# Two expert layers: first stage on a ring of eight tiles loaded by pairs, and 18 weighted row sums per layer moved to the value stage

## Chip, cores and metric

The kernel runs on one core of one Trainium2 chip. The metric is the device time of one execution in microseconds; the figure before is the median of three runs.

## What is computed

The program is a chain of a hybrid first layer, an even layer (sparse attention), an expert layer, an MLA layer, a second expert layer and a final norm, all over 256 tokens of width 1024. The change touches the two expert layers alone. Cut to them, the reference is:

```
def peer_ffn(h, w_q, sub_keys, u_tab, v_tab):      # u_tab, v_tab: 128*128 experts x 1024
    q = (xc @ w_q).reshape(t, 8, 2, 128)
    sc = einsum('thpc,hpnc->thpn', q, sub_keys)
    v_half, i_half = top_k(sc, 16)                 # 16 of 128 first keys, 16 of 128 second keys
    top_s, pos = top_k(all 16*16 sums, 16)         # 16 experts for each of 8 heads
    g = softmax(top_s)
    act = gelu(einsum('thkd,td->thk', u_tab[expert], xc))
    return einsum('thk,thkd->td', g * act, v_tab[expert])
```

## The kernel before

An expert layer (`expert_layer`, once with i = 0 and once with i = 1) treats 192 of the 256 tokens densely and 64 by gathers.

**Dense tokens, first stage.** For each of 128 first keys, TensorE multiplies the key's tile of u (128 x 1024 floats, 0.5 MB) with the tokens: `experts`, L2401, eight matmuls of 192 columns into half a bank. For each pair of keys ScalarE applies the gelu and stores into `hidden` (L2504). VectorE meanwhile finds the 16 experts of each head, and after key 80 the weights begin: VectorE writes one-hots (`one_hots`, L2280 to L2286), TensorE multiplies them (`weights`, L2296, 32 products of 6 tokens over keys 0 to 79 of `hidden`), VectorE multiplies the result into `hidden` (`weigh`, L2305).

**Dense tokens, value stage.** For each of 128 tiles of v (0.5 MB), ScalarE rounds the tile (`tile_hi`, L2491 and L2523) and the key's row of `hidden` (`w_parts`, L2495, L2496), VectorE makes the two remainders (`value_rest`: `tile_lo` L2729, `w_parts` L2732), and TensorE does ten matmuls of 512 columns (`values`: L2428, L2429, L344 to L346). Over the first 72 tiles, 24 weight products of the other 48 keys lie among them, one behind each third tile, with their one-hots and weighings on VectorE.

**The 64 other tokens.** GpSimd gathers 128 times 0.5 MB through eight buffers (L2245): 64 u rows, with each of which VectorE makes a dot product (`row_dot`, L2253), and 64 v rows, each of which VectorE weights and adds (`row_value`, L2259, called a weighted row sum or sum below). `take(upto)` places them in VectorE's order, up to a count: `TAKEN[3]` of the 128 are done when the first stage ends, `TAKEN[4]` after value tile index 72 of the loop, and the rest is spread evenly up to index `LAST_TAKE`. A gather waits until the buffer's last row is used.

**Loads.** SyncE issues all tiles in order into a ring of four slots in `wbuf`. A u tile's load waits until the key four before is used by TensorE (semaphore `used`); a v tile's load waits until VectorE has made the remainder of the tile four before (`lo_done`). `tile_hi` and `tile_lo` lie behind the ring in `wbuf` and aren't used in the first stage.

**Order at the turn of the stages.** On ScalarE, behind the gelu of keys 124 and 125, v tiles 0 and 1 are rounded. When the last key is used and the weighing is done, the hidden rows of four tiles are rounded, then comes the last gelu, then v tiles 2 and 3.

Every engine works through its own queue in order, written out by hand; only semaphores tie them together.

Of the kernel before, what the change touches and what calls it, by code (L numbers as in the profile page):

```python
# [119 lines left out]
def build(nc, ins, out):  # L120
    with ExitStack() as ctx:
# [24 lines left out]
        def carver():  # L146
# [1960 lines left out]
def expert_layer(nc, g, ins, i):  # L2107
# [112 lines left out]

    def sync(sp):
# [8 lines left out]
        load_table(sp, U, M_U, lo_done, used)  # L2230
# [3 lines left out]
        load_table(sp, V, M_V, used, lo_done)  # L2234
# [73 lines left out]
    FIRST_WEIGHING, FIRST_LOOPS, FIRST_LOOP = FIRST_KEYS // STEP, 2, 20  # L2308
    FIRST_AT = {j: n for n, j in enumerate(j for j in range(FIRST_LOOP) if j % 5 < 4)}
# [3 lines left out]
    TAKEN, LAST_TAKE = (16, 30, 36, 86, 92), 118  # L2313
    EXPS_AT, ACTS_AT, ACTS = (16, 30), (46, 51), (slice(0, 48), slice(48, SHARED))
# [21 lines left out]
    def tensor(pe):  # L2336
# [627 lines left out]
```

## Time and profile before

| | |
|---|---|
| median of 3 runs | 2057.09 us (2050.85 to 2057.55) |
| the profiled execution | 2056.46 us, span 2054.4 us |
| TensorE busy (PE), weight loads (PEld) | 97%, 87% |
| VectorE, ScalarE, GpSimd busy | 78%, 42%, 18% |
| moved over the span | 511.18 MB, mean 249 GB/s |
| the 4096 records of L2401 | 683.8 us busy |
| the 128 weighted row sums, L2259 | 164.2 us busy, 1283 ns each |
| u and v loads | 256 of 512.0 KB each, median 6.3 and 4.7 us to landing |

The time of an execution is a little over the span, which is from the first to the last instruction. An instruction's duration can overlap the next one on its engine, so the cost of one in a row of many is the distance from start to start.

### The profile page before, as it was taken

Reading aid. Unit: us, or ns where it says so; the run is one execution under the profiler, and the core shown is the slowest. Engines: PE = TensorE matmul, PEld = TensorE weight load, DVE = VectorE, ACT = ScalarE, POOL = GpSimd, SP = SyncE. Lnnn points to the kernel's source line nnn. Section 1 sums busy time; section 2 is a strip of 40 time slices with the busy share of each in tenths; the row PEclk is TensorE's granted clock in tenths of the full one; section 3 lists DMA queues with packets and bytes.
Section 4 is the critical chain, followed back from the end, with each engine's and each line's share of the span. In section 5 each row is a group of like instructions: output and inputs, shape, how many; then the busy total and the mean of one; then the engine's idle time right before and its main releaser. Section 6 shows DMA issues by size and latency. Waiting matters only on the chain.

```text
span 2054.4 us, 35333 instructions
## 1 busy us (share of the span) xinstructions
PE 2001.3 (97%) x12408; PEld 1792.1 (87%) x12408; DVE 1607.6 (78%) x3302; ACT 863.2 (42%) x1655; POOL 377.9 (18%) x262
## 2 busy tenths in 40 slices
PE   8999999999999999999999999999999999999998
PEld 6888887879999999988888787899999999888886
DVE  6899886865798159868889977649951996988997
ACT  6557555555101100056566666531101001655665
POOL 0000000000024225500125200000341453011460
PEclk9999999999999999999999999999999999999999
DMA  6554335415389979976779853335997899777895
GB/s 252 207 182 186 113 122 161 155 36 196 125 337 361 351 253 391 374 245 233 235 249 395 326 197 124 106 125 201 396 372 270 326 380 347 234 235 235 322 397 201
DMA packets 132636, 511.18 MB, mean 249 GB/s; under 512 B 15005, under 2 KB 15133, under 8 KB 129857
## 3 DMA queue, kind: packets, MB, share of 16 engines
q1 hardware_dynamic: 95680, 375.81, 51.7%
q0 software_dynamic: 36864, 134.23, 17.1%
q8 instruction: 48, 0.79, 0.1%
q14 instruction: 44, 0.35, 0.0%
HBM read 508.94 MB, written 1.05 MB: 248 GB/s over the span
## 4 chain that ended last, share of the span: by engine, by line
PE 66%; DVE 17%; DMA 2%; ACT 2%; issue 2%; SPq 0%; DVEq 0%; ACTq 0%
PE bank L2401 22%; PE bank L344 10%; PE bank L346 10%; PE bank L345 10%; PE bank L2428 5%; PE bank L2429 5%; DVE e_gbuf L2253 3%; DVE x_tok L2259 3%; DVE e_hot_first L2286 2%; DVE e_hidden L2305 2%; DMA wbuf<-in_peer_v 2%; PE bank L2296 1%; DVE e_is_first L2280 1%; DVE e_hot_second L2282 1%; DVE tile_lo L274 1%
## 5 line engine op out<-in xcount | busy, mean ns | idle before, releaser
L2401 PE MATMUL bank<-h_dense,wbuf 128*128 128x192 f32 x4096 | 683.8, 327 | 3.2 <-ACT e_stage L2477 2.4
L2401 PEld LDWEIGHTS bank<-h_dense,wbuf 128*128 128x128 f32 x4096 | 663.4, 190 | 6.2 <-issue 4.3
L2523 ACT ACTIVATE tile_hi<-wbuf 128x1024 fp32r<-128x1024 f32 x248 | 263.8, 1064 | 225.6 <-PE bank L346 139.9
L2729 DVE TENSOR_TENSOR tile_lo<-wbuf,tile_hi 128x1024 fp32r<-128x1024 f32 x256 | 312.9, 1222 | 44.2 <-ACT tile_hi L2491 34.3
L2504 ACT ACTIVATE e_hidden<-bank 128x384 f32<-128x384 f32 x128 | 62.9, 492 | 609.9 <-PE bank L2401 609.9
L2245 POOL DMA_INDIRECT e_gbuf<-in_peer_v,e_row_at x128 | 224.4, 1753 | 489.4 <-DVE x_tok L2259 465.5
L2245 POOL DMA_INDIRECT e_gbuf<-in_peer_rows,e_row_at x128 | 151.4, 1183 | 476.5 <-DVE e_dots L2253 261.3
L2428 PE MATMUL bank<-tile_hi,w_parts 128*128 128x512 f32 x512 | 205.4, 401 | 4.0 <-DVE w_parts L2732 3.8
L274 DVE TENSOR_TENSOR tile_lo<-wbuf,tile_hi 128x1024 fp32r<-128x1024 f32 (+2 forms) x117 | 140.5, 1212 | 76.3 <-ACT tile_hi L266 75.5
L2429 PE MATMUL bank<-tile_lo,w_parts 128*128 128x512 f32 x512 | 200.1, 391 | 0.0
L344 PE MATMUL bank<-tile_hi,w_parts 128*128 128x512 f32 x512 | 199.7, 390 | 0.0
L345 PE MATMUL bank<-tile_lo,w_parts 128*128 128x512 f32 x512 | 199.6, 390 | 0.0
L346 PE MATMUL bank<-tile_hi,w_parts 128*128 128x512 f32 x512 | 199.5, 390 | 0.0
L355 PE MATMUL bank<-a_parts,tile_hi 128*128 128x512 f32 x512 | 181.0, 399 | 0.0
L2253 DVE CUSTOM_DVE_ANT_0 e_gbuf<-e_gbuf,x_gathered 128x1024 f32<-128x1024 f32 x128 | 152.9, 1222 | 17.2 <-DMA e_gbuf<-in_peer_rows,e_row_at 16.8
L2259 DVE SCALAR_TENSOR_TENSOR x_tok<-e_gbuf,e_acts,x_tok 128x1024 f32<-128x1024 f32 x128 | 164.2, 1283 | 1.8
L266 ACT ACTIVATE tile_hi<-wbuf 128x1024 fp32r<-128x1024 f32 (+2 forms) x117 | 122.1, 1047 | 64.5 <-PE bank L346 57.5
L354 PE MATMUL bank<-a_parts,tile_hi 128*128 128x256 f32 x512 | 144.2, 282 | 0.4 <-DVE tile_hi L681 0.2
L2239 POOL MEMSET x_tok<- 64x1024 f32 x2 | 1.9, 950 | 660.9 <-DVE e_stage L2560 660.9
L2428 PEld LDWEIGHTS bank<-tile_hi,w_parts 128*128 128x128 f32 x512 | 96.2, 188 | 26.7 <-DVE w_parts L2732 7.6
L561 ACT ACTIVATE tile_hi<-wbuf 128x512 fp32r<-128x512 f32 x144 | 90.3, 632 | 69.4 <-PE bank L355 65.8
L681 DVE TENSOR_TENSOR tile_hi<-wbuf,tile_hi 128x512 fp32r<-128x512 f32 x144 | 98.5, 688 | 24.5 <-ACT tile_hi L561 23.6
(396 smaller groups left out, 3472.2 us busy)
## 6 DMA issues: line engine op xcount, KB each, us to landing
wbuf<-in_peer_u SPq DMA_DIRECT2D x256, 512.0 KB, 6.3
wbuf<-in_peer_v SPq DMA_DIRECT2D x256, 512.0 KB, 4.7
wbuf<-in_w_in SPq DMA_DIRECT2D x16, 2048.0 KB, 7.8
wbuf<-in_peer_q SPq DMA_DIRECT2D x32, 512.0 KB, 3.8
wbuf<-in_hyb_in SPq DMA_DIRECT2D x16, 512.0 KB, 3.6
wbuf<-in_mla_uq SPq DMA_DIRECT2D x9, 512.0 KB, 3.4
wbuf<-in_mla_in SPq DMA_DIRECT2D x8, 528.0 KB, 4.6
wbuf<-in_w_v SPq DMA_DIRECT2D x2, 2048.0 KB, 7.2
```

The costliest lines, as they stand in the source:

```text
L344: nc.tensor.matmul(out, hi[:, cols], other_hi, start=start, stop=False, **kw)
L345: nc.tensor.matmul(out, hi[:, cols], other_lo, start=False, stop=False, **kw)
L346: return nc.tensor.matmul(out, lo[:, cols], other_hi, start=False, stop=stop, **kw)
L355: return nc.tensor.matmul(out, hi[:, cols], parts, start=False, stop=stop, skip_group_check=True)
L2245: nc.gpsimd.indirect_dma_start(out=gbuf[:, b, :], out_offset=None, in_=(U_ROWS if n < SHARED else V_ROWS)[:, :], in_offset=bass.IndirectOf ...
L2253: nc.vector.tensor_tensor_reduce(out=gbuf[:, n % GBUFS, :], in0=gbuf[:, n % GBUFS, :], in1=x_gathered[:, :], scale=1.0, scalar=0.0, op0=AL ...
L2259: nc.vector.scalar_tensor_tensor(out=x[:, 1, :], in0=gbuf[:, n % GBUFS, :], scalar=acts[:, n:n + 1], in1=x[:, 1, :], op0=ALU.mult, op1=ALU ...
L2401: last = nc.tensor.matmul(bank[:, j // 2 % 2, j % 2 * S:j % 2 * S + DENSE], ring[:, slot, k * P:(k + 1) * P], h_dense[:, k, :], start=(k = ...
L2428: nc.tensor.matmul(sums(1, c), both, tile_hi[:, slot, cols], start=False, stop=False, skip_group_check=True)
L2429: last = nc.tensor.matmul(sums(1, c), both, tile_lo[:, slot, cols], start=False, stop=False, skip_group_check=True)
L2523: nc.scalar.activation(tile_hi[:, slot, 0:D], ring[:, slot, 0:D], ACT.Copy).then_inc(hi_done, 1)
L2729: nc.vector.tensor_tensor(tile_lo[:, slot, 0:D], ring[:, slot, 0:D], tile_hi[:, slot, 0:D].bitcast(F32), ALU.subtract).then_inc(lo_done, 1)
```

## The change

1. `deep` is a ring of eight u tiles over the memory of the old ring and of `tile_hi`. `load_pair` fills two neighbouring tiles with one transfer of 1 MB, `experts` waits for it at every even key, and `load_first` refills a pair when both its keys are used. V tiles keep the ring of four; the first four of them are loaded behind keys 120, 122, 124 and 126.
2. At the turn ScalarE waits for the weighing behind the gelu of keys 124 and 125, then rounds v tile 0, its hidden row, v tile 1, its hidden row; tiles 2 and 3 with their rows follow the last gelu.
3. The 32 weight products of the first stage lie behind three of four keys from key 80 to 111 and behind two of three from key 112 to 122, before behind four of five keys from 80 to 119.
4. `TAKEN` places 68 of the gathered rows in the first stage instead of 86: of the 64 weighted row sums, 4 instead of 22. Value tiles to index 72 get 10 instead of 6, the rest 50 instead of 36, over 49 indices instead of 46.

```diff
+            "deep": wbuf[:, 0:2, :].rearrange("p w (j c) -> p (w j) c", c=TILE),
...
-    def load_table(sp, table, base, before, free):
-
-        for j in range(STEP):
-            sp.wait_ge(before if j < SLOTS else free, base + j - SLOTS + 1)
-            load_slot(sp, table, j, (base + j) % SLOTS)
-        with sp.Fori(1, ROUNDS) as r:
-            for j in range(STEP):
-                sp.wait_ge(free, STEP * r + base + j - SLOTS + 1)
-                load_slot(sp, table, STEP * r + j, (base + j) % SLOTS)
+    def load_pair(sp, a, p):
+        sp.dma_start(deep[:, 2 * p:2 * p + 2, 0:D], U[bass.ds(a, 2), :, :].rearrange("a p c -> p a c")).then_inc(ring_loaded[p], DMA)
+
+    def load_first(sp):
+        for p in range(SLOTS):
+            ring_slots = [s % SLOTS for s in (2 * p, 2 * p + 1)]
+            if p < SLOTS // 2:
+                sp.wait_ge(lo_done, max(last_before(s) for s in ring_slots + [p]) + 1)
+            else:
+                sp.wait_ge(lo_done, last_before(p) + 1)
+                sp.wait_ge(used, max(last_before(s) for s in ring_slots) + 1)
+            load_pair(sp, 2 * p, p)
+        with sp.Fori(1, ROUNDS) as r:
+            for p in range(SLOTS):
+                sp.wait_ge(used, STEP * r + M_U - STEP + 2 * p + 2)
+                load_pair(sp, STEP * r + 2 * p, p)
...
+    def load_second(sp):
+        for a in range(SLOTS):
+            slot = (M_V + a) % SLOTS
+            sp.wait_ge(used, M_U + LAST_ROUND + 2 * slot + 1)
+            load_value(sp, a, slot)
+        for a in range(SLOTS, STEP):
+            sp.wait_ge(lo_done, M_V + a - SLOTS + 1)
+            load_value(sp, a, (M_V + a) % SLOTS)
...
-    FIRST_WEIGHING, FIRST_LOOPS, FIRST_LOOP = FIRST_KEYS // STEP, 2, 20
-    FIRST_AT = {j: n for n, j in enumerate(j for j in range(FIRST_LOOP) if j % 5 < 4)}
+    FIRST_WEIGHING, FIRST_LOOPS, FIRST_LOOP = FIRST_KEYS // STEP, 2, 2 * STEP
+    FIRST_AT = {j: n for n, j in enumerate(j for j in range(FIRST_LOOP) if j % 4 < 3)}
+    FIRST_END = FIRST_KEYS + FIRST_LOOPS * FIRST_LOOP
+    END_AT = {j: FIRST_LOOPS * len(FIRST_AT) + n for n, j in enumerate(j for j in range(12) if j % 3 < 2)}
...
-    TAKEN, LAST_TAKE = (16, 30, 36, 86, 92), 118
-    EXPS_AT, ACTS_AT, ACTS = (16, 30), (46, 51), (slice(0, 48), slice(48, SHARED))
+    TAKEN, LAST_TAKE = (16, 30, 36, 68, 78), 121
+    EXPS_AT, ACTS_AT, ACTS = (16, 30), (51, 61), (slice(0, 48), slice(48, SHARED))
...
-            slot = (M_U + j) % SLOTS
-            pe.wait_ge(ring_loaded[slot], DMA * (width // SLOTS * q + (M_U + base + j) // SLOTS + 1))
+            slot = (base + j) % STEP
             if j % 2 == 0:
+                pe.wait_ge(ring_loaded[slot // 2], DMA * (width // STEP * q + pairs_loaded(slot // 2) + (base + j) // STEP + 1))
...
             act.wait_ge(used, M_U + 2 * f + 2)
-            if f == NKEYS // 2 - 1:
-                act.wait_ge(weighted, 2 + NGROUPS[0])
-                for a in range(SLOTS):
-                    hidden_rounded(a, a)
...
             if f >= NKEYS // 2 - 2:
-                for a in range(2):
-                    rounded_v(2 * (f - NKEYS // 2 + 2) + a)
+                if f == NKEYS // 2 - 2:
+                    act.wait_ge(weighted, 2 + NGROUPS[0])
+                for e in range(2):
+                    a = 2 * (f - NKEYS // 2 + 2) + e
+                    rounded_v(a)
+                    hidden_rounded(a, a)
```

Line numbers of the changed kernel are larger: L2729 becomes L2768, L2732 L2771, L2259 L2291, L2504 L2539.

VectorE in the value stage of the first expert layer, near tile 90, before (x_tok is the weighted row sum):

```order
L2729 TENSOR_TENSOR tile_lo<-wbuf,tile_hi 128x1024 [waits hi_done]
L2732 TENSOR_TENSOR w_parts<-e_hidden,w_parts 128x192 [waits e0_w_hi_done]
L2259 SCALAR_TENSOR_TENSOR x_tok<-e_gbuf,e_acts,x_tok 128x1024 [waits gather_used,gathered1]
L2729 TENSOR_TENSOR tile_lo<-wbuf,tile_hi 128x1024 [waits hi_done]
L2732 TENSOR_TENSOR w_parts<-e_hidden,w_parts 128x192 [waits e0_w_hi_done]
L2729 TENSOR_TENSOR tile_lo<-wbuf,tile_hi 128x1024 [waits hi_done]
L2732 TENSOR_TENSOR w_parts<-e_hidden,w_parts 128x192 [waits e0_w_hi_done]
```

The same place in the changed kernel:

```order
L2768 TENSOR_TENSOR tile_lo<-wbuf,tile_hi 128x1024 [waits hi_done]
L2771 TENSOR_TENSOR w_parts<-e_hidden,w_parts 128x192 [waits e0_w_hi_done]
L2291 SCALAR_TENSOR_TENSOR x_tok<-e_gbuf,e_acts,x_tok 128x1024 [waits gather_used,gathered7]
L2768 TENSOR_TENSOR tile_lo<-wbuf,tile_hi 128x1024 [waits hi_done]
L2771 TENSOR_TENSOR w_parts<-e_hidden,w_parts 128x192 [waits e0_w_hi_done]
L2291 SCALAR_TENSOR_TENSOR x_tok<-e_gbuf,e_acts,x_tok 128x1024 [waits gather_used,gathered0]
```

Before, some tiles have no sum ahead of them (36 sums over 46 tiles); in the changed kernel each of the tiles 74 to 122 has one, and tile 123 has two.

ScalarE at the turn of the stages in the first expert layer, before, from the gelus up to that of keys 124 and 125 (eleven in one row) to the last rounding ahead of the value loop (left out are the hidden rows of tiles 1 to 3):

```order
L2504 ACTIVATE e_hidden<-bank 128x384 [waits used] x11
L2491 ACTIVATE tile_hi<-wbuf 128x1024 [waits ring_loaded0]
L2491 ACTIVATE tile_hi<-wbuf 128x1024 [waits ring_loaded1]
L2495 ACTIVATE w_parts<-e_hidden 128x192 [waits e0_weighted,used]
L2496 ACTIVATE w_parts<-e_hidden 128x64
...
L2504 ACTIVATE e_hidden<-bank 128x384
L2491 ACTIVATE tile_hi<-wbuf 128x1024 [waits ring_loaded2]
L2491 ACTIVATE tile_hi<-wbuf 128x1024 [waits ring_loaded3]
```

And in the changed kernel:

```order
L2539 ACTIVATE e_hidden<-bank 128x384 [waits used]
L2530 ACTIVATE tile_hi<-wbuf 128x1024 [waits ring_loaded0,used,e0_weighted]
L2534 ACTIVATE w_parts<-e_hidden 128x192
L2535 ACTIVATE w_parts<-e_hidden 128x64
L2530 ACTIVATE tile_hi<-wbuf 128x1024 [waits ring_loaded1,used]
L2534 ACTIVATE w_parts<-e_hidden 128x192
L2535 ACTIVATE w_parts<-e_hidden 128x64
L2539 ACTIVATE e_hidden<-bank 128x384 [waits used]
```

The hidden rows of tiles 0 and 1 have moved ahead of the last gelu and no longer wait for the last key; the wait for the weighing moved up with them.

## Rows read from the trace of the kernel before

**Rows 1.** Timeline of ScalarE, the gelu of a pair of keys: start us, duration us.
```profile
542.75 0.49 ACT L2504 ACTIVATE e_hidden<-bank 128x384 f32<-128x384 f32 x1 [3.37 <-PE bank L2401]
...
589.55 0.49 ACT L2504 ACTIVATE e_hidden<-bank 128x384 f32<-128x384 f32 x1 [4.71 <-PE bank L2401]
...
741.74 0.49 ACT L2504 ACTIVATE e_hidden<-bank 128x384 f32<-128x384 f32 x1 [4.71 <-PE bank L2401]
748.49 0.49 ACT L2504 ACTIVATE e_hidden<-bank 128x384 f32<-128x384 f32 x1 [6.25 <-PE bank L2401]
...
778.62 0.49 ACT L2504 ACTIVATE e_hidden<-bank 128x384 f32<-128x384 f32 x1 [5.22 <-PE bank L2401]
...
880.29 0.49 ACT L2504 ACTIVATE e_hidden<-bank 128x384 f32<-128x384 f32 x1 [4.71 <-PE bank L2401]
...
1396.72 0.49 ACT L2504 ACTIVATE e_hidden<-bank 128x384 f32<-128x384 f32 x1 [3.37 <-PE bank L2401]
...
1734.48 0.49 ACT L2504 ACTIVATE e_hidden<-bank 128x384 f32<-128x384 f32 x1 [4.84 <-PE bank L2401]
```

**Rows 2.** Chain that ended last, then timeline of TensorE, first stage.
```profile
592.56 8.18 DMA wbuf<-in_peer_u
...
830.33 0.62 PE L2296 MATMUL bank<-e_hot_first,e_hot_second 128*128 128x80 f16 x12 [0.31 <-DVE e_hot_first L2286]
```

**Rows 3.** Timeline of TensorE at the turn, both layers; idle time stands in brackets.
```profile
888.08 0.70 PE L2428 MATMUL bank<-tile_hi,w_parts 128*128 128x512 f32 x1 [2.62 <-DVE w_parts L2732]
...
892.07 0.57 PE L2296 MATMUL bank<-e_hot_first,e_hot_second 128*128 128x48 f16 x16
892.49 0.47 PE L2428 MATMUL bank<-tile_hi,w_parts 128*128 128x512 f32 x1
...
1740.63 0.50 PE L2428 MATMUL bank<-tile_hi,w_parts 128*128 128x512 f32 x1 [0.99 <-DVE w_parts L2732]
...
1743.87 0.47 PE L2428 MATMUL bank<-tile_hi,w_parts 128*128 128x512 f32 x1
```

**Rows 4.** Timeline of TensorE: first matmuls of tiles 73, 127; 73, 114, 127.
```profile
1067.83 0.39 PE L2428 MATMUL bank<-tile_hi,w_parts 128*128 128x512 f32 x1
...
1192.56 0.39 PE L2428 MATMUL bank<-tile_hi,w_parts 128*128 128x512 f32 x1
...
1919.21 0.39 PE L2428 MATMUL bank<-tile_hi,w_parts 128*128 128x512 f32 x1
...
2012.14 0.39 PE L2428 MATMUL bank<-tile_hi,w_parts 128*128 128x512 f32 x1
...
2042.45 0.39 PE L2428 MATMUL bank<-tile_hi,w_parts 128*128 128x512 f32 x1
```

**Rows 5.** Windows: length, busy PE, PEld, DVE, ACT, POOL; clock, DMA share, GB/s.
```profile
888.00:892.50 4.50, 4.42 (x27) 3.40 (x27) 4.50 (x11) 3.31 (x9) 0.00 (x0) 0.62 0.81 304
...
1100.00:1131.00 31.00, 31.00 (x138) 25.63 (x137) 30.53 (x37) 19.07 (x40) 16.44 (x11) 1.00 1.01 394
...
1917.00:2034.00 117.00, 116.91 (x514) 95.94 (x513) 115.36 (x141) 74.51 (x153) 60.70 (x29) 1.00 0.95 357
```

**Rows 6.** Timeline of VectorE: a weighing cycle, tile 73, tiles 84 and 85.
```profile
1046.48 0.56 DVE L2305 SCALAR_TENSOR_TENSOR e_hidden<-bank,e_hidden 128x384 f32<-128x384 f32 x1 [0.95 <-PE bank L2296]
...
1915.52 0.35 DVE L2732 TENSOR_TENSOR w_parts<-e_hidden,w_parts 128x192 fp32r<-128x192 f32 x1
...
1939.39 1.23 DVE L2729 TENSOR_TENSOR tile_lo<-wbuf,tile_hi 128x1024 fp32r<-128x1024 f32 x1
...
1940.80 1.29 DVE L2259 SCALAR_TENSOR_TENSOR x_tok<-e_gbuf,e_acts,x_tok 128x1024 f32<-128x1024 f32 x1
1941.99 1.23 DVE L2729 TENSOR_TENSOR tile_lo<-wbuf,tile_hi 128x1024 fp32r<-128x1024 f32 x1
```

**Rows 7.** Chain that ended last, value stage of the first expert layer.
```profile
1068.40 7.04 DMA wbuf<-in_peer_v
...
1075.53 1.07 ACT tile_hi L2523
```

More of the change, by code:

```diff
@@ L2229, in sync @@
             load_tile(sp, g, ins, M_Q + j)
-        load_table(sp, U, M_U, lo_done, used)
+        load_first(sp)
         if i == 0:
@@ L2233, in sync @@
                 sp.sem_clear(handle)
-        load_table(sp, V, M_V, used, lo_done)
+        load_second(sp)
     def gpsimd(pool):
@@ L2394, in experts @@
         def experts(q, width, base, j):
-            slot = (M_U + j) % SLOTS
-            pe.wait_ge(ring_loaded[slot], DMA * (width // SLOTS * q + (M_U + base + j) // SLOTS + 1))
+            slot = (base + j) % STEP
             if j % 2 == 0:
+                pe.wait_ge(ring_loaded[slot // 2], DMA * (width // STEP * q + pairs_loaded(slot // 2) + (base + j) // STEP + 1))
+                if base + j >= LAST_ROUND:
+                    pe.sem_inc(ring_loaded[slot // 2], NKEYS // STEP * DMA)
                 pe.wait_ge(bank_free, width // 2 * q + (base + j) // 2 + 1)
             for k in range(KT):
-                last = nc.tensor.matmul(bank[:, j // 2 % 2, j % 2 * S:j % 2 * S + DENSE], ring[:, slot, k * P:(k + 1) * P], h_dense[:, k, :],
+                last = nc.tensor.matmul(bank[:, j // 2 % 2, j % 2 * S:j % 2 * S + DENSE], deep[:, slot, k * P:(k + 1) * P], h_dense[:, k, :],
                                         start=(k == 0), stop=(k == KT - 1))
@@ L2416, in tensor @@
                     weights(pe, 0, len(FIRST_AT) * q + FIRST_AT[j], FIRST_AT[j] % 2)
-        for j in range(NKEYS - FIRST_KEYS - FIRST_LOOPS * FIRST_LOOP):
-            experts(0, STEP, FIRST_KEYS + FIRST_LOOPS * FIRST_LOOP, j)
+        for j in range(NKEYS - FIRST_END):
+            experts(0, STEP, FIRST_END, j)
+            if j in END_AT:
+                weights(pe, 0, END_AT[j], END_AT[j] % 2)
         def values(q, width, base, j, ends=False):
@@ L2489, in rounded_v @@
             slot = (M_V + a) % SLOTS
+            act.wait_ge(used, M_U + NKEYS - SLOTS + slot + 1)
             act.wait_ge(ring_loaded[slot], DMA * ((M_V + a) // SLOTS + 1))
```

12 lines of the change are left out of this document (10 added, 2 removed).

## Prediction

> **What bounds the kernel now.** I read the stage windows first, then followed each stage's pace by one instruction that recurs in it, then looked only at where the pace breaks. TensorE is the bound almost everywhere, so a term counts only where TensorE waits.
>
> First stage: the gelu (L2504) starts once per pair of keys. Its starts at 542.75 and 589.55 us are nine pairs apart, 5.20 us each [rows 1]. From 748.49 to 778.62 lie five pairs and eight weight products of L2296: 30.13 - 26.00 = 4.13, or 0.516 us each [rows 1]. The pair from 741.74 to 748.49 takes 6.75, which is 5.20 + 0.52 + 1.02 for turning the picks, work that stays. So 61 pairs should take 61 x 5.20 + 32 x 0.516 + 1.02 = 334.7 us. They take 880.29 - 542.75 = 337.5 in the first expert layer and 1734.48 - 1396.72 = 337.8 in the second [rows 1]. The stalls are thus 2.8 and 3.1 us. Two kinds make them: a late u tile (the chain that ended last goes through a landing of 8.18 us at 592.56) and late one-hots from VectorE (TensorE idle 0.31 before 830.33) [rows 2].
>
> Turn from first to value stage: TensorE idles 2.62 us in the first layer, and the value tile behind it takes 892.49 - 888.08 = 4.41 us; in the second layer 0.99, and 1743.87 - 1740.63 = 3.24 [rows 3].
>
> Value stage: from tile 73 to tile 114 of the second layer, 41 tiles, TensorE needs 2012.14 - 1919.21 = 92.9 us, 2.267 each [rows 4]. VectorE is the engine to watch: it is busy 115.36 of 117 us in the last third of this stage [rows 5]. A tile with a row sum takes it 1941.99 - 1939.39 = 2.60 us, and the sum alone 1941.99 - 1940.80 = 1.19 (1.20 below) [rows 6]. A tile without one is 1.40. So VectorE is slower than TensorE on a tile with a sum (by 0.33) and faster on one without (by 0.87). What saves TensorE is a lead: the parts of tile 73 are ready at 1915.52 + 0.35 = 1915.87 [rows 6], and TensorE wants them at 1919.21 [rows 4], 3.34 us later. Before, 36 sums lie over 46 tiles and the lead is used up only near the end: tiles 73 to 127 should take 54 x 2.267 = 122.4 and take 124.7 in the first layer (1192.56 - 1067.83) and 123.2 in the second (2042.45 - 1919.21) [rows 4]. That is 2.3 and 0.8 us lost.
>
> **Part one, the ring and the pairs.** A slot of four is refilled when its key is used, so a load has three keys, 7.8 us, to land; 8.18 didn't fit [rows 2]. A pair in a ring of eight has six keys, 15.6 us. The pair is one transfer of 1 MB instead of two of 0.5; even at twice the 8.18 us it would be late by under 1 us. Its issue costs SyncE less, and nothing queues behind it there except the next pair. I take the u stalls as gone.
>
> **Part two, fewer sums in the first stage.** A weight product there now comes each 4/3 key (3.98 us) and later each 1.5 keys, before each 1.25 keys (3.77). VectorE's share falls from 50/32 = 1.56 sums per product to 1. Its wait for nothing and TensorE's 0.31 at 830.33 [rows 2] say that it was just over budget; 0.56 x 1.20 = 0.67 us less work in 0.2 us more time clears it. With part one: gain 2.8 + 3.1 = **5.9 us**, bounds 3 (one of the two kinds stays; these rows don't split them, so I take half) and 5.9, since no more stall exists.
>
> **Part three, the turn.** The v loads now leave after keys 120, 122, 124 and 126, and ScalarE rounds v tiles 0 and 1 and their hidden rows right behind the gelu of keys 124 and 125, 5.2 us before the last key ends. ScalarE needs 0.49 for the gelu [rows 1] and 1.07 for a tile [rows 7], VectorE 1.4 more, so both tiles are ready before TensorE is. The new wait for the weights stands ahead of this on ScalarE; behind it are the last gelu and the v roundings. It asks for product 31, which is made after key 122, three keys earlier, so it costs nothing; were it late, the gain of the turn shrinks by that much. A usual value tile with its weight product is 2.27 plus 892.49 - 892.07 = 0.42 [rows 3], 2.69. So the turn costs 2.62 + 4.41 - 2.69 = 4.3 and 0.99 + 3.24 - 2.69 = 1.5 us; I keep 0.2 each for the switch of code. Gain 4.1 + 1.3 = **5.4 us**, bounds 3.6 (the two idles alone) and 5.8. Most of the first layer's excess is the clock: granted 0.62 of full in 888.00:892.50 after the long idle [rows 5], a mix of the 1.2 and 2.4 GHz levels. With no idle nothing drops it.
>
> **Part four, 18 more sums in the value stage.** Four go to tiles 0 to 73, where weight products leave VectorE 0.95 us of waiting in a cycle of three tiles [rows 6]. Ten sums over 24 cycles, never two in one: 0.25 of each is taken from the lead, which the next cycle's 0.95 gives back, so nothing. If it didn't come back, it would be 10 x 0.25 = 2.5 us per layer. The other 14 are the price. The order listing has one sum ahead of each of tiles 74 to 122, and two ahead of tile 123. VectorE needs 49 x 2.60 + 3.80, TensorE 50 x 2.267: behind by 49 x 0.333 + 1.53 = 17.9 us. The lead pays 3.3, so TensorE loses 14.6 us per layer. Less what it loses already: 14.6 - 2.3 + 14.6 - 0.8 = **26.1 us**. What covered a sum, the tiles without one between, is gone. Behind tile 123 no sum follows, but VectorE's later slack can't give time back to TensorE.
>
> The lower bound of this term is a sum hidden by something I don't see; I find no row for that, since every sum takes 1.20. The upper bound is the transfers. A v tile and a gather in 2.60 us are 1.049 MB, or 403 GB/s. The window 1100.00:1131.00 moved 394 GB/s at a share of 1.01 [rows 5], and a v tile then needed 7.04 us to land [rows 7], where the ring of four allows 4 x 2.60 less 1.07 and 1.40, 7.9. At 394, a tile takes 2.66: 0.06 x 42 tiles = 2.5 us per layer more, 5 in all. I take 1.
>
> The Trainium skill (DMA: Bandwidth & Descriptors, Where 436 GB/s comes from) says that for transfers between HBM and SBUF the HBM side binds at about 358 GB/s per core. By that rule a tile of 1.049 MB would take 2.93 us and the two tails some 28 us more than my sum. The row with 394 GB/s speaks against it here.
>
> **Sum.** -5.9 - 5.4 + 26.1 + 1 = +15.8. The profiled execution is 2056.46 us (span 2054.4), the median 2057.09, 0.6 above it. 2056.5 + 15.8 = 2072.3, and 2072.9 beside the median: I say 2073.
>
> **Rivals.**
> A, as above, VectorE paces both tails: with the bounds of the other terms 2057.1 + 26.1 - 11.7 = 2071 to 2057.1 + 26.1 + 5 - 6.6 = 2082, and some 4 us below for what my reading of the lead and of the sum may be off. Chance 0.77.
> B, the transfers pace the tails. For it: the share of 1.01. Against: 394 GB/s is 2% short of 403, eight gather buffers smooth it, and VectorE's slower pace asks for less per us in the v ring. At 394 GB/s: 2077. At the 357 GB/s that 1917.00:2034.00 moved [rows 5], which wasn't asked for more, 2.94 us per tile: 0.34 x 42 x 2 = 28 more, 2100. Chance 0.11, mostly its lower half.
> C, TensorE's clock falls in the tails, since TensorE now pauses 0.33 us in every tile. The tile after the long idle took 892.07 - 888.08 = 3.99 instead of 2.27 [rows 3]. That is 1.4 more than VectorE's 2.60; one tile in four of the 39 without lead gives 14 us per layer: 2100. Against: the pause before 830.33 [rows 2] and a last stretch at granted 1.00 [rows 5]. Chance 0.03. The Trainium skill (TensorE: Matmul & The Clock Gate, A second HAM failure mode) describes a kernel whose frequent short idles made the clock oscillate.
> D, the other side: a row sum in the tail costs VectorE less than 1.20. With t for the sum, 49 tiles of 1.40 + t and one of 1.40 + 2t against 50 x 2.267 + 3.3 make TensorE's loss 51t - 46.7 per layer. The rest of the change gives 11.3, and before's loss 3.1, so the balance is at 7.2 per layer, t = 1.06. Below that the kernel is faster: at t = 1.0 by some 6 us, 2051. For it: VectorE would have to be slowed now by something that the change thins out, such as TensorE's or the transfers' traffic. Against: the tail before, with and without a sum, keeps to 2.60 and 1.40 [rows 6], and gathers become denser, not rarer. Within 0.3%: 0.04, faster: 0.05.
>
> **Numbers.** 0.3% (about 6 us) is what a measurement here tells from no change. A gives 2067 to 2082; the range adds B's nearer half and a little of the ground between A and D: 2064 to 2084. Outside are the far half of B, C and D, 0.05 + 0.03 + 0.09, so under 2 in 10. Faster 0.05, within 0.3% 0.05 (D's 0.04 and an edge of A), slower 0.90.
>
> **What would show it.** First stages: 61 pairs in 334.7 us, no idle named after u. Turn: an idle under 0.3 us and a first tile of 2.7. Tail: tiles 84 to 122 at 2.60 us, each waiting on VectorE, tile 127 of the second layer 137 us after tile 73, VectorE without idle between. Wrong if tail tiles stay at 2.27, if they wait on ScalarE and through it on v landings over 7.9 us (B), if the granted clock dips there (C), or if the first stage shows stalls of a new kind.

## The result, and the profile after

The changed kernel takes 2076.07 us (median of five runs, 2072.78 to 2080.81); the kernel before takes 2057.55 (five runs, 2050.85 to 2061.82). The ratio is 1.0091, with a 95% interval of 1.0075 to 1.0108: slower by 18.5 us. The forecast was 2073, in a range of 2064 to 2084.

The page of the changed kernel: span, then busy time, share and instructions of each engine.

```profile
span 2074.0 us, 34807 instructions
...
PE 2020.3 (97%) x12408; PEld 1789.3 (86%) x12408; DVE 1606.2 (77%) x3302; ACT 861.3 (42%) x1655; POOL 353.4 (17%) x262
```

The totals say next to nothing: the same instructions stand in another order. So here too the stages are laid out by instructions that recur. First the gelu of the changed kernel, timeline of ScalarE, against [rows 1]; the rounding and the hidden row that now stand between the last two gelus are shown with it.

```profile
545.78 0.49 ACT L2539 ACTIVATE e_hidden<-bank 128x384 f32<-128x384 f32 x1 [3.37 <-PE bank L2437]
...
880.64 0.49 ACT L2539 ACTIVATE e_hidden<-bank 128x384 f32<-128x384 f32 x1 [4.61 <-PE bank L2437]
881.02 1.05 ACT L2530 ACTIVATE tile_hi<-wbuf 128x1024 fp32r<-128x1024 f32 x1
881.97 0.35 ACT L2534 ACTIVATE w_parts<-e_hidden 128x192 fp32r<-128x192 f32 x1
...
885.84 0.49 ACT L2539 ACTIVATE e_hidden<-bank 128x384 f32<-128x384 f32 x1 [2.02 <-PE bank L2437]
...
1406.48 0.49 ACT L2539 ACTIVATE e_hidden<-bank 128x384 f32<-128x384 f32 x1 [3.37 <-PE bank L2437]
...
1741.34 0.49 ACT L2539 ACTIVATE e_hidden<-bank 128x384 f32<-128x384 f32 x1 [4.61 <-PE bank L2437]
```

61 pairs take 880.64 - 545.78 = 334.86 us in either layer; they took 337.5 and 337.8 [rows 1]. V tile 0 is rounded at 881.02, 4.5 us before TensorE wants it.

Timeline of TensorE of the changed kernel: value tiles 0, 1 and 73 of the first layer, tiles 92 and 93, the tile with two sums ahead of it (123) and tile 127; then tiles 73 and 127 of the second layer. They answer to [rows 3, 4].

```profile
885.50 0.53 PE L2466 MATMUL bank<-tile_hi,w_parts 128*128 128x512 f32 x1
...
887.95 0.57 PE L2328 MATMUL bank<-e_hot_first,e_hot_second 128*128 128x48 f16 x16
888.37 0.47 PE L2466 MATMUL bank<-tile_hi,w_parts 128*128 128x512 f32 x1
...
1063.71 0.39 PE L2466 MATMUL bank<-tile_hi,w_parts 128*128 128x512 f32 x1
...
1109.83 0.50 PE L2466 MATMUL bank<-tile_hi,w_parts 128*128 128x512 f32 x1
...
1112.43 0.50 PE L2466 MATMUL bank<-tile_hi,w_parts 128*128 128x512 f32 x1
...
1192.14 0.47 PE L2466 MATMUL bank<-tile_hi,w_parts 128*128 128x512 f32 x1 [1.47 <-DVE w_parts L2771]
...
1201.33 0.39 PE L2466 MATMUL bank<-tile_hi,w_parts 128*128 128x512 f32 x1
...
1924.49 0.39 PE L2466 MATMUL bank<-tile_hi,w_parts 128*128 128x512 f32 x1
...
2062.06 0.39 PE L2466 MATMUL bank<-tile_hi,w_parts 128*128 128x512 f32 x1
```

The turn has no idle, and the first value tile takes 888.37 - 885.50 = 2.87 us (before 4.41 and 3.24). Tiles 73 to 127 take 137.6 us in each layer, against 124.7 and 123.2 [rows 4]. Tiles 92 and 93 are 2.60 apart, not 2.27.

Waits of the changed kernel in 1925:2062, the second layer's tail: engine, what it waited for, total us, times, longest; and then its windows there (columns as in [rows 5]).

```profile
ACT tile_hi L2562 <- DMA wbuf<-in_peer_v: 52.9, 46, 2.5
...
PEld bank L2466 <- DVE w_parts L2771: 17.0, 37, 0.7
...
DVE tile_lo L2768 <- ACT tile_hi L2562: 0.3, 1, 0.3
```
```profile
1920.00:2062.00 142.00, 138.91 (x561) 101.88 (x560) 140.31 (x165) 78.74 (x162) 71.20 (x43) 1.00 0.92 355
...
1950.00:2025.00 75.00, 73.87 (x289) 52.02 (x289) 74.96 (x87) 42.40 (x88) 47.78 (x30) 1.00 1.03 409
```

Here the engine that waits for nothing is VectorE: 0.3 us in 137, and 74.96 of 75.00 busy. ScalarE waits long for v tiles, but VectorE waits for ScalarE only once, for 0.3 us, so those 52.9 us cost nothing here. TensorE's weight loads wait for VectorE 37 times.

**Where 19.6 us between the two profiled executions went.** First stages 334.86 - 337.55 and 334.86 - 337.76: -5.6. From the last full gelu to value tile 1: 7.73 in both layers, where it was 12.19 and 9.39: -6.1. Tiles 1 to 73: 175.34 and 175.42, before 175.34 twice: +0.1. Tails: +12.9 and +14.3. This is +15.6. Another 3.0 come from code ahead of the first expert layer which the change doesn't touch: the expert stage starts at 535.08 instead of 532.05, after a stretch in which the two kernels' windows (before first, changed second) show another granted clock.

```profile
400.00:450.00 50.00, 42.67 (x293) 33.02 (x292) 36.81 (x129) 28.41 (x93) 0.00 (x0) 0.86 0.06 19
```
```profile
400.00:450.00 50.00, 42.56 (x278) 32.93 (x277) 35.96 (x128) 28.57 (x93) 0.00 (x0) 0.80 0.06 18
```

The last 1 us is spread over the rest. Below, stages are therefore compared and not spans alone; "tail" is tile 73 to tile 127 by their first matmuls. The sums given for a tail are those that `TAKEN` places behind index 72; one more, the last of those before, also lies behind the parts of tile 73 in every kernel.

### The profile page after: what moved, and what is told of

Read it like the earlier page. It is cut to its first block, busy times and chain, and to the rows that moved or that the text cites. A ratio compares the mean times of both kernels' runs of the same rounds, so it can differ in the third digit from the quotient of the medians.

```text
span 2074.0 us, 34807 instructions
## 1 busy us (share of the span) xinstructions
PE 2020.3 (97%) x12408; PEld 1789.3 (86%) x12408; DVE 1606.2 (77%) x3302; ACT 861.3 (42%) x1655; POOL 353.4 (17%) x262
## 4 chain that ended last, share of the span: by engine, by line
PE 70%; DVE 12%; issue 5%; ACT 2%; DMA 1%; DVEq 0%; ACTq 0%; SPq 0%
PE bank L2437 32%; PE bank L345 8%; PE bank L347 8%; PE bank L346 8%; DVE x_tok L2291 5%; PE bank L2466 4%; PE bank L2467 3%; PE bank L2328 2%; DVE w_parts L2771 1%; DMA wbuf<-in_peer_v 1%; DVE tile_lo L275 1%; PE bank L2420 1%; DVE tile_lo L2768 1%; PE bank L1573 0%; ACT tile_hi L267 0%
## 5 line engine op out<-in xcount | busy, mean ns | idle before, releaser
L2768 DVE TENSOR_TENSOR tile_lo<-wbuf,tile_hi 128x1024 fp32r<-128x1024 f32 x256 | 311.4, 1216 | 23.1 <-ACT tile_hi L2530 17.6
L2539 ACT ACTIVATE e_hidden<-bank 128x384 f32<-128x384 f32 x128 | 62.7, 490 | 607.7 <-PE bank L2437 607.7
L2277 POOL DMA_INDIRECT e_gbuf<-in_peer_v,e_row_at x128 | 205.2, 1603 | 489.3 <-DVE x_tok L2291 441.2
L2277 POOL DMA_INDIRECT e_gbuf<-in_peer_rows,e_row_at x128 | 146.1, 1141 | 534.9 <-DVE e_dots L2285 321.9
L2466 PE MATMUL bank<-tile_hi,w_parts 128*128 128x512 f32 x512 | 213.4, 417 | 6.0 <-DVE w_parts L2771 3.4
L345 PE MATMUL bank<-tile_hi,w_parts 128*128 128x512 f32 x512 | 199.7, 390 | 0.0
L347 PE MATMUL bank<-tile_hi,w_parts 128*128 128x512 f32 x512 | 199.4, 389 | 0.0
L2291 DVE SCALAR_TENSOR_TENSOR x_tok<-e_gbuf,e_acts,x_tok 128x1024 f32<-128x1024 f32 x128 | 163.3, 1275 | 0.3
L2337 DVE SCALAR_TENSOR_TENSOR e_hidden<-bank,e_hidden 128x480 f32<-128x480 f32 (+1 forms) x112 | 68.4, 611 | 79.3 <-PE bank L2328 79.2
```

What stands on the lines that cost most here:

```text
L345: nc.tensor.matmul(out, hi[:, cols], other_hi, start=start, stop=False, **kw)
L347: return nc.tensor.matmul(out, lo[:, cols], other_hi, start=False, stop=stop, **kw)
L2277: nc.gpsimd.indirect_dma_start(out=gbuf[:, b, :], out_offset=None, in_=(U_ROWS if n < SHARED else V_ROWS)[:, :], in_offset=bass.IndirectOf ...
L2291: nc.vector.scalar_tensor_tensor(out=x[:, 1, :], in0=gbuf[:, n % GBUFS, :], scalar=acts[:, n:n + 1], in1=x[:, 1, :], op0=ALU.mult, op1=ALU ...
L2466: nc.tensor.matmul(sums(1, c), both, tile_hi[:, slot, cols], start=False, stop=False, skip_group_check=True)
L2768: nc.vector.tensor_tensor(tile_lo[:, slot, 0:D], ring[:, slot, 0:D], tile_hi[:, slot, 0:D].bitcast(F32), ALU.subtract).then_inc(lo_done, 1)
```

## Experiments

Ten kernels, in three groups on one chip each; the kernel before took 2059.02, 2058.42 and 2057.88 us in them. Unless the text says otherwise, a diff is against the changed kernel. `TAKEN` counts gathers, of which 64 are the dot products: 86 means 22 sums in the first stage.

**Only the sums put back.**

```diff
-    TAKEN, LAST_TAKE = (16, 30, 36, 68, 78), 121
-    EXPS_AT, ACTS_AT, ACTS = (16, 30), (51, 61), ...
+    TAKEN, LAST_TAKE = (16, 30, 36, 86, 92), 118
+    EXPS_AT, ACTS_AT, ACTS = (16, 30), (46, 53), ...
```

> The changed kernel with the old placing of the row sums (86 gathered rows in the first stage, 92 by value tile 72, the rest by index 118); the ring of eight, the pairs and the new turn stay. Theory V (VectorE is late in the tail because of the moved sums): the tail, tile 73 to tile 127, goes back to 123 to 125 us per layer from 137.7, the first stage keeps its 334.8 us for 61 pairs, the turn its 5.2 us, and the kernel is 11 us faster than before, 2046. Rival X (the 1 MB pairs or the deeper ring cost something themselves): it stays at or above 2057, with new idle time in the first stage or the turn.

Measured: 2049.11 us, ratio 0.9958 (0.9940 to 0.9976). Tails 125.8 and 124.5, 61 pairs 334.76 in both layers, although the first stage has its 22 sums again. The loss is in part four alone, and ring, pairs and turn are a gain. The time is 3 us above the 2046 that was expected: the first tail lies 0.8 us above its range, and the first value tile of the second layer took 4.12 us, where that of the first layer took 2.85. Timeline of this kernel, TensorE and then ScalarE at that place:

```profile
1734.00 0.57 PE L2328 MATMUL bank<-e_hot_first,e_hot_second 128*128 128x48 f16 x16 [1.12 <-DVE e_hot_first L2318]
```
```profile
1729.95 1.06 ACT L2530 ACTIVATE tile_hi<-wbuf 128x1024 fp32r<-128x1024 f32 x1 [2.69 <-DMA wbuf<-in_peer_v]
```

V tile 1 landed late, its remainder stands ahead of the next one-hots on VectorE, and TensorE's weight product waited 1.12 us for these.

**Only the sums moved.** The kernel before, with parts one to three left out. Against before:

```diff
-    TAKEN, LAST_TAKE = (16, 30, 36, 86, 92), 118
-    EXPS_AT, ACTS_AT, ACTS = (16, 30), (46, 51), ...
+    TAKEN, LAST_TAKE = (16, 30, 36, 68, 78), 121
+    EXPS_AT, ACTS_AT, ACTS = (16, 30), (51, 60), ...
```

> The kernel before with only the placing of the row sums from the change (68, 78, index 121). Theory V: the tails take 137.7 us instead of 124.7 and 123.2, so +27, and the one-hot waits of the first stage (about half of 5.9) go: -3. Sum +24, 2081. Rival X: within a few us of 2057.

Measured: 2080.21, ratio 1.0102 (1.0087 to 1.0118). Tails 138.4 and 137.6: the old ring and the old turn pay the same price. 61 pairs take 336.04 and 335.42, so fewer sums alone take 1.5 and 2.3 of the 2.8 and 3.1 us of stalls in the first stage. These are mostly the late one-hots: the waits of TensorE's weight loads for them fell from 2.5 us to 0.5 in both layers. In the second layer, those for u tiles fell too, from 1.2 us to 0.2, with the old ring and fewer gathers. TensorE, second layer, tiles 73 and 127:

```profile
1925.92 0.39 PE L2428 MATMUL bank<-tile_hi,w_parts 128*128 128x512 f32 x1
...
2063.54 0.39 PE L2428 MATMUL bank<-tile_hi,w_parts 128*128 128x512 f32 x1
```

**Half of each sum.** This kernel weights and adds only half of each gathered row; gathers and v tiles are all loaded.

```diff
-        nc.vector.scalar_tensor_tensor(out=x[:, 1, :], in0=gbuf[:, n % GBUFS, :], ..., in1=x[:, 1, :],
+        nc.vector.scalar_tensor_tensor(out=x[:, 1, 0:CHUNK], in0=gbuf[:, n % GBUFS, 0:CHUNK], ..., in1=x[:, 1, 0:CHUNK],
```

> The changed kernel, but each weighted row sum treats only columns 0 to 511 of the 1024, so the output lacks the other half of those sums; all gathers stay. Theory V: VectorE needs about 0.6 us less per sum, 2.0 us per tile with a sum, less than TensorE's 2.27, so no tile waits and the tail takes 122.4 to 123.5 us: about -29, 2047. Rival B (the transfers, 403 GB/s asked in the tail, pace it, VectorE's work is only beside them): at 2.27 us per tile the same bytes would be 462 GB/s, which no window has shown, so the tail stays above 2.5 us per tile at first and ScalarE waits for v tiles; a tail of 130 us or more.

Measured: 2064.5, ratio 1.0029 (1.0018 to 1.0039), tails 132.3 and 132.4. Windows of this kernel in the second layer's tail, then timelines of ScalarE and VectorE there:

```profile
1950.00:2025.00 75.00, 74.35 (x297) 53.21 (x296) 63.84 (x90) 43.04 (x88) 51.94 (x30) 1.00 1.03 409
```
```profile
1978.29 1.06 ACT L2562 ACTIVATE tile_hi<-wbuf 128x1024 fp32r<-128x1024 f32 x1 [1.10 <-DMA wbuf<-in_peer_v]
...
1980.79 1.06 ACT L2562 ACTIVATE tile_hi<-wbuf 128x1024 fp32r<-128x1024 f32 x1 [1.04 <-DMA wbuf<-in_peer_v]
```
```profile
1978.24 0.75 DVE L2291 SCALAR_TENSOR_TENSOR x_tok<-e_gbuf,e_acts,x_tok 128x512 f32<-128x512 f32 x1
...
1979.38 1.23 DVE L2768 TENSOR_TENSOR tile_lo<-wbuf,tile_hi 128x1024 fp32r<-128x1024 f32 x1 [0.40 <-ACT tile_hi L2562]
```

VectorE now has 63.84 us of work in 75, so it needs about 2.2 us per tile and waits 0.40 for ScalarE, which waits over 1 us for each v tile. At 409 GB/s a tile with its gather, 1.049 MB, takes 2.56 us. TensorE keeps to this: by its timeline, tiles 90 to 118 of the second layer are (2032.11 - 1960.46) / 28 = 2.56 us apart.

```profile
1960.46 0.50 PE L2466 MATMUL bank<-tile_hi,w_parts 128*128 128x512 f32 x1
...
2032.11 0.50 PE L2466 MATMUL bank<-tile_hi,w_parts 128*128 128x512 f32 x1
```

This is the bound that comes next, and it lies 0.04 us under VectorE's 2.60. With VectorE relieved, the tails fall by 5 us, not to 122: 2064.5 is 17 us above the 2047 that was expected, and the tails are those that the rival of this run named, 130 us or more with ScalarE waiting for v tiles. So VectorE sets the pace of the changed kernel, but some 10 of the 15 us that each of its tails loses to TensorE's pace would stay if VectorE alone were faster.

**The sums back, and six more between weighings.** 22 sums in the first stage, 12 in tiles 0 to 73, 30 in the tail.

```diff
-    TAKEN, LAST_TAKE = (16, 30, 36, 68, 78), 121
+    TAKEN, LAST_TAKE = (16, 30, 36, 86, 98), 118
```

(`ACTS_AT` is (46, 53), as in the first experiment.)

> The changed kernel with 86 gathered rows in the first stage, 12 sums by value tile 72 and only 30 in the tail (to index 118). Theory V: VectorE needs 46 x 1.40 + 30 x 1.20 = 100.4 us where TensorE needs 104.3, so the lead is never used up and the tail takes 122.4 to 123.0 us; with the first stage and the turn of the change the kernel is 14 us faster than before, 2043. Rival X: at or above 2057. Rival Y (the first stage can't hold 86 rows without the one-hot waits even with the products farther apart): 3 us of stalls in the first stages, 2046.

Measured: 2048.03, ratio 0.9942 (0.9927 to 0.9957). This is 5 us above the 2043 expected. Tails 125.4 and 126.9, not under 123. Windows of this kernel's second tail, and a rounding in it:

```profile
1914.00:2034.00 120.00, 119.09 (x512) 94.67 (x511) 109.01 (x133) 72.71 (x152) 31.16 (x22) 1.00 0.88 314
```
```profile
1955.53 1.06 ACT L2562 ACTIVATE tile_hi<-wbuf 128x1024 fp32r<-128x1024 f32 x1 [3.16 <-DMA wbuf<-in_peer_v]
```

VectorE has 11 us of slack in 120, and still TensorE loses 3 to 4.5. What is late are v tiles: ScalarE waits up to 3.16 us for one, VectorE for ScalarE (10.8 us in all), TensorE for VectorE. A count of VectorE's work alone misses this.

**Fourteen more sums between weighings.** The 14 sums come out of the tail (50 to 36) into tiles 0 to 73 (10 to 24, one in each weighing cycle); first stage and turn are those of the changed kernel.

```diff
-    TAKEN, LAST_TAKE = (16, 30, 36, 68, 78), 121
+    TAKEN, LAST_TAKE = (16, 30, 36, 68, 92), 118
```

> The changed kernel with its 68 gathered rows in the first stage, but 24 of the 60 sums among tiles 0 to 72 (one in each cycle of three, instead of 10) and 36 in the tail, to index 118, as before. Theory V (the loss is where the sums lie, not that they are in the value stage): the tail goes back to about 125.5 us as in the run with the old placing; a cycle of three tiles has 1.15 us of waiting on VectorE for a sum of 1.20, so tiles 1 to 73 take 175.3 to 178 us. Sum 2049 to 2054. Rival Z (18 more sums in the value stage cost about 27 us wherever they lie, since stage and bytes are the same): 2070 or more.

Measured: 2049.85, ratio 0.9960 (0.9945 to 0.9974). Tiles 1 to 73 take 175.34 and 175.36, as without these sums; tails 124.7 and 128.4, the second 3 us above the 125.5 expected. TensorE, second layer, tiles 1 and 73:

```profile
1736.01 0.47 PE L2466 MATMUL bank<-tile_hi,w_parts 128*128 128x512 f32 x1
...
1911.37 0.39 PE L2466 MATMUL bank<-tile_hi,w_parts 128*128 128x512 f32 x1
```

The 14 sums cost nothing between weighings, and their absence takes 12.9 and 9.1 us off the tails. In the second layer they used up some of the lead, though: the parts of tile 73 are ready 2.87 us before TensorE starts it, and 3.33 in the first layer. In that tail VectorE waits 6.0 us for ScalarE, which waits up to 4.15 us for a v tile.

**Seven sums out of the tail.** A dose between the two: 43 sums in the tail.

```diff
-    TAKEN, LAST_TAKE = (16, 30, 36, 68, 78), 121
+    TAKEN, LAST_TAKE = (16, 30, 36, 68, 85), 121
```

> The changed kernel with 85 instead of 78 gathered rows done by value tile 72, so 17 sums among tiles 0 to 72 and 43 in the tail (to index 121). VectorE's bound by the prediction's sum: 7 sums of 1.20 less in the tail, a loss of 14.6 - 8.4 = 6.2 us per layer instead of 14.6, tail 128.6 us instead of 137.7 at best; transfers at 410 GB/s ask for 7 x 1.28 us less than the 132.3 us of the run with half sums, 123.4, and stay below. So 128.6 to 130 us in each layer, -17 us to the changed kernel: 2059, as fast as before. Rival (the tail is set by transfers alone, about 5 us above their bound): a drop of 9 us in each tail only if bytes set it; then ScalarE waits for v tiles at every tile.

Measured: 2058.53, ratio 0.9996 (0.9984 to 1.0008), tails 130.9 and 129.8. From 50 sums to 43 a tail gets 7.3 us shorter on average, 1.04 per sum, near VectorE's 1.20. One tail lies in the expected range and one 0.9 above it. With these seven sums placed between weighings, the changed kernel is level with the one before: what the sums cost has sunk to what the other parts gain.

**The sums earlier, spread to tile 124.** 22 sums in the first stage, 22 in tiles 0 to 73, 20 in the tail.

```diff
-    TAKEN, LAST_TAKE = (16, 30, 36, 68, 78), 121
+    TAKEN, LAST_TAKE = (16, 30, 36, 86, 108), 124
```

(`ACTS_AT` again (46, 53).)

> The changed kernel with 86 gathered rows in the first stage, 22 sums among tiles 0 to 72 and 20 in the tail, to index 124. Theory VB (two bounds in the tail: VectorE's 2.60 us for a tile with a sum, and transfers at 410 GB/s or a late v tile): with 20 sums both have room, and the tail takes 122.4 to 123 us in both layers, 5 us less in all than with the old placing: 2044. Theory V alone (transfers don't matter): the same as the run with 30 sums in the tail, 2048. Rival Z: no difference to it either.

Measured: 2045.6, ratio 0.9946 (0.9929 to 0.9963). Tails 122.4 and 123.4, so the first is at TensorE's own pace and the second 0.4 us above the range.

**The old order at the turn.** The first experiment, with ScalarE's old order for the hidden rows; against that kernel:

```diff
+            if f == NKEYS // 2 - 1:
+                act.wait_ge(weighted, 2 + NGROUPS[0])
+                for a in range(SLOTS):
+                    hidden_rounded(a, a)
...
-                if f == NKEYS // 2 - 2:
-                    act.wait_ge(weighted, 2 + NGROUPS[0])
                 for e in range(2):
-                    a = 2 * (f - NKEYS // 2 + 2) + e
-                    rounded_v(a)
-                    hidden_rounded(a, a)
+                    rounded_v(2 * (f - NKEYS // 2 + 2) + e)
```

> The changed kernel with the old placing of the sums, and the turn on ScalarE as before: the four hidden rows are rounded only when the last key is used, ahead of the last gelu. The early v loads stay. If the early rounding is what removed the idle of the turn: TensorE idles 1.0 to 1.2 us there in both layers (0.25 to 0.4 for the rounding, 0.35 for VectorE's remainder, the rest handovers), and the clock stays up: +2 to +3 us to the run with the old placing, 2051 to 2052. If only the early v loads removed it: no difference.

Measured: 2051.69, ratio 0.9968 (0.9956 to 0.9980), 2.6 above the first experiment, which ran on another chip. TensorE at value tile 0 of both layers:

```profile
883.00 0.50 PE L2466 MATMUL bank<-tile_hi,w_parts 128*128 128x512 f32 x1 [0.99 <-DVE w_parts L2771]
...
1731.50 0.50 PE L2466 MATMUL bank<-tile_hi,w_parts 128*128 128x512 f32 x1 [1.30 <-DVE w_parts L2771]
```

In the first layer the new loads with the old order give 6.15 + 3.23 = 9.38 us from the last full gelu to value tile 1; the kernel before needed 12.19, the new order 7.73. So 2.8 of the 4.5 us gained there don't need ScalarE's new order. Of these 2.8, 1.2 are the tile behind the idle, which took 4.41 us in before and 3.23 here (on this tile more below). In the second layer the new loads with the old order gain nothing: 6.46 + 3.23 = 9.69, against 9.39 in the kernel before. V tile 1 landed late there too, and ScalarE waited 3.13 us for it.

**The pairs as two transfers each.** The first experiment with a ring of eight but transfers of 0.5 MB:

```diff
-        sp.dma_start(deep[:, 2 * p:2 * p + 2, 0:D], U[bass.ds(a, 2), :, :]...).then_inc(ring_loaded[p], DMA)
+        for e in range(2):
+            sp.dma_start(deep[:, 2 * p + e, 0:D], U[bass.ds(a + e, 1), :, :]...).then_inc(ring_loaded[p], DMA)
```

> The changed kernel with the old placing of the sums, and each pair of u tiles loaded by two transfers of 0.5 MB issued together instead of one of 1 MB; the ring of eight stays. If the depth of the ring removed the stalls of the first stage: 61 pairs still take 334.8 us and the time is that of the run with the old placing within 2 us. If the size of the transfer did: stalls on u tiles come back, up to 3 us.

Measured: 2047.87, ratio 0.9951 (0.9936 to 0.9966). ScalarE's gelu, pairs 1 and 62 of the first layer:

```profile
539.99 0.49 ACT L2538 ACTIVATE e_hidden<-bank 128x384 f32<-128x384 f32 x1 [3.37 <-PE bank L2436]
...
874.75 0.49 ACT L2538 ACTIVATE e_hidden<-bank 128x384 f32<-128x384 f32 x1 [4.71 <-PE bank L2436]
```

334.76, as with pairs. So the size of the transfers isn't what took the stalls away. What is left is the depth of the ring and the wider spacing of the weight products, which this kernel has too; no run has one of these without the other.

Five kernels have the same 36 sums in the tail, to the same index: before, the first experiment, the one with fourteen more sums between weighings, the old turn and this one. Their ten tails still take from 123.2 to 128.4 us. In the shortest VectorE waits 1.9 us in all for ScalarE to round v tiles, in the two longest 6.0 and 6.5.

**Eighty gathers in the first stage.** 80 gathers (16 sums) in the first stage, 22 sums between weighings, 26 in the tail.

```diff
-    TAKEN, LAST_TAKE = (16, 30, 36, 68, 78), 121
-    EXPS_AT, ACTS_AT, ACTS = (16, 30), (51, 61), ...
+    TAKEN, LAST_TAKE = (16, 30, 36, 80, 102), 124
+    EXPS_AT, ACTS_AT, ACTS = (16, 30), (48, 56), ...
```

> 80 gathered rows in the first stage, 22 sums among tiles 0 to 72 and 26 in the tail, to index 124. Against the run with 86, 22 and 20: fewer gathers near the end of the second layer's first stage, so v tile 1 isn't late there and the first value tile takes 2.9 us instead of 3.7; the tail has 6 more sums and 6 more gathers, VectorE needs 51 x 1.40 + 26 x 1.20 = 102.6 us where TensorE needs 115.6, so 122.4 to 124 us. Sum within 2 us of 2045.6. Rival: if v landings grow with every added gather, the tail takes 125 us or more and the run is 4 us or more slower.

Measured: 2045.04, ratio 0.9929 (0.9912 to 0.9945), the lowest median of all kernels here; the intervals of the kernels with 20 and with 30 sums in the tail overlap this one. Windows of the second tail, and TensorE at tiles 73 and 127:

```profile
1904.00:2027.00 123.00, 123.00 (x544) 101.90 (x543) 109.18 (x136) 75.18 (x159) 31.22 (x19) 1.00 0.84 300
```
```profile
1904.00 0.39 PE L2466 MATMUL bank<-tile_hi,w_parts 128*128 128x512 f32 x1
...
2026.40 0.39 PE L2466 MATMUL bank<-tile_hi,w_parts 128*128 128x512 f32 x1
```

TensorE is busy for all of the 123 us, and both tails take 122.40, which is 54 x 2.267. VectorE has 109 us of work, as in the kernel with 30 sums in the tail, but in 123 us instead of 120, and the transfers move 300 GB/s instead of 314. V tiles still land late. Waits of this kernel in the same window:

```profile
DVE tile_lo L2768 <- ACT tile_hi L2562: 11.7, 14, 2.1
```

The difference is in the room for this. By the counts in the two expectations, VectorE has 115.6 - 102.6 = 13.0 us to spare up to its last sum here, and 104.3 - 100.4 = 3.9 with 30 sums, and the lead of 3.3 comes on top in both. 11.7 us of waits fit into 16.3; 10.8 are 3.6 more than 7.2, where the tail lost 4.5, so the count is a rough one. The kernel is some 13 us under the kernel before and 31 under the changed one. The first value tile of the second layer took 3.83 us where 2.9 was expected; this miss is taken up below.

## Why the prediction was right, step by step

**Part one and two: first stages, -5.9 forecast, -5.6 measured.** The mechanism holds: no idle is named after u any more, and 334.86 is 0.1 above what was worked out. Fewer sums alone took 1.5 and 2.3 us (only the sums moved), mostly late one-hots; how the whole splits between one-hots and u tiles isn't shown more closely, since the u waits of the second layer fell with the sums too. But ring and spacing took all of both away without fewer sums: with 22 sums back in the first stage, the pairs stay at 334.76. Weight products and sums are spaced differently there than before, so this doesn't say whether the new spacing or the deeper ring took the one-hot waits. It does say that moving 18 sums out bought nothing that ring and spacing hadn't.

**Part three: the turn, -5.4 forecast, -6.1 measured.** The new wait for the weights cost nothing, as forecast. The first value tile takes 2.86, next to the 2.69 + 0.2 of the forecast, and the way from the last full gelu to value tile 0 shrank by 2.92 and 1.29 us, which is 0.3 in each layer beyond the idle shown in [rows 3]. That is nearly all of the 0.7. What the step said of the clock held for the profiled execution of the kernel before, and not for every one. With the sums moved alone, the first layer has an idle of 2.56 us at the same place, but the tile behind it takes 886.36 - 883.13 = 3.23. Timeline of TensorE of that kernel, and its window over this tile, to be held against the 0.62 in [rows 5]:

```profile
883.13 0.50 PE L2428 MATMUL bank<-tile_hi,w_parts 128*128 128x512 f32 x1 [2.56 <-DVE w_parts L2732]
...
886.36 0.47 PE L2428 MATMUL bank<-tile_hi,w_parts 128*128 128x512 f32 x1
```
```profile
883.00:886.40 3.40, 3.02 (x27) 2.25 (x27) 3.40 (x8) 3.16 (x8) 0.00 (x0) 1.00 0.87 305
```

Nearly the same idle was followed by a granted clock of 0.62 once and of 1.00 once. So the 1.2 us by which the tile behind the idle was longer (4.41 against 3.23) need not be there in every execution.

**Part four: the tails, +26.1 and +1 forecast, +27.2 measured.** Tiles 84 to 122 are 2.60 us apart but for two steps of 2.82 and 2.69, each behind VectorE; the tails take 137.6 where 54 x 2.267 + 14.6 = 137.0 was worked out. These two steps, the 3.99 behind tile 122 (3.80 in the sum) and the 2.39 or 2.35 behind that make up the 0.6; the 1 us taken for the transfers isn't in it, since VectorE didn't wait for them. The 14 sums and their gathers in a row were the whole price, and the ten between weighings cost 0.1. This step carried the sign of the result, and the runs bear it out from both sides: sums alone moved give +13.6 and +14.4 in the tails, sums alone put back take 11.9 and 13.1 off. That VectorE and not the transfers set the pace is in part luck: by the 2.56 us per tile measured with half sums, the two bounds lay 0.04 us apart, and the step had put the transfers at 2.66, above VectorE, only to count 1 us of the 5 that this gives.

One sentence of this step was too simple: it took the 2.3 and 0.8 us that before lost in its tails for VectorE's used-up lead. With VectorE at 109 of 120 us busy (the sums back and six more), the tails still lose 3.0 and 4.5 us, by late v tiles. So VectorE's count alone doesn't explain what before lost. In the changed kernel the error didn't show, since VectorE set the pace throughout and a late tile hid behind it.

**The rivals.** B, transfers pace the tails, fell as the cause of this result, since VectorE waits for ScalarE only once in the second tail, for 0.3 us; but it was far nearer than its chance of 0.11 suggests. At 409 GB/s the transfers need 2.56 us per tile, 0.04 below VectorE. The 357 GB/s of its upper half were, as suspected, only what had been asked for. The Trainium skill (DMA: Bandwidth & Descriptors, Where 436 GB/s comes from) puts the HBM side's limit at about 358 GB/s per core. By that figure a tile is estimated at 2.93 us, and the two tails at some 28 us more than the sum; the 409 GB/s over 75 us in two kernels speak against it for this kernel, which runs on one core. No run here shows two cores at once. C, the clock, fell: TensorE's tiles take 0.33 us longer than at its own pace, and its granted clock stays at 1.00 over 142 us. D, a cheaper sum, fell: timeline of VectorE of the changed kernel, first layer's tail, where a sum takes 1110.90 - 1109.71 = 1.19 and a tile with its sum 1112.31 - 1109.71 = 2.60, as in [rows 6]:

```profile
1109.71 1.27 DVE L2291 SCALAR_TENSOR_TENSOR x_tok<-e_gbuf,e_acts,x_tok 128x1024 f32<-128x1024 f32 x1
1110.90 1.21 DVE L2768 TENSOR_TENSOR tile_lo<-wbuf,tile_hi 128x1024 fp32r<-128x1024 f32 x1
...
1112.31 1.27 DVE L2291 SCALAR_TENSOR_TENSOR x_tok<-e_gbuf,e_acts,x_tok 128x1024 f32<-128x1024 f32 x1
```

**Beyond the terms.** The result lies 3.1 us above 2073. The terms leave -0.2 of it (15.6 against 15.8), and 0.5 is the median of before, which came out at 2057.55 instead of 2057.09. The other 2.8 are not the change's own in anything that the traces show: the profiled executions differ by 3.0 ahead of the first expert stage, where the programs are alike.

**What stays open.** Why v tile 1 of the second layer lands late. ScalarE waits 2.3 to 2.7 us for it with 80 or 86 gathers in the first stage and the new turn, and the first value tile takes 3.7 to 4.1 us. In the four kernels with 68 it waits 0.8 us, and the tile takes 2.84 to 2.86. In the first layer of all these kernels it doesn't wait at all. More gathers at the end of the first stage fit the difference between the kernels, but not that between the layers: with 86, the last four leave 13.5 to 8.3 us before the first value tile in both. No run settles it. Open is also whether the deeper ring or the wider spacing freed the first stage, and how much of the turn's gain is the clock over many executions.

## What to carry to other kernels

Before side work is moved on a helper engine that feeds the bound engine, count both engines in each repeating unit at the place where it goes: here a sum is free in a weighing cycle with 0.95 us of waiting, and in a tail with a sum on every tile each tile loses 0.33 us once a lead of 3.3 is gone. Spread such work over the places with slack first, and leave the helper some slack, since it also takes up late transfers: here 16.3 us of room in a tail held 11.7 us of waits, and 7.2 didn't hold 10.8. Measure the next bound before counting on the whole gain: here transfers stood 0.04 us per tile below VectorE.

## What was not expected of the hardware

- One core moved 409 GB/s for 75 us, at a share of 1.03, with v tiles issued by SyncE and gathers by GpSimd.
- An idle of 2.6 us on TensorE lowered the granted clock to 0.62 once and not at all once; idles of 0.99 and 1.30 us, and tiles that each take 0.33 us longer than TensorE's own pace for 100 us, never did.
- Code that is the same in all kernels, up to the first expert stage, ended between 528.4 and 536.0 us in the twelve profiled executions, with granted clocks from 0.80 to 0.86 in 400:450. That is more than several of the terms sized here, so terms were read from stages, and only the sums from medians.
